# First feed-forward product of a two-layer encoder kernel: tokens stationary and 512 weight columns moving, stage borders by token tile, low weight halves in place

## The chip, the cores and the metric

The kernel runs on one core of one Trainium2 chip. The metric is the device time of one execution in microseconds (us), as the median of the runs; smaller is better. TensorE is called PE in the rows, VectorE DVE, ScalarE ACT, GpSimd POOL and SyncE SP; SPq is SP's DMA queue.

## What is computed

Two layers over 256 tokens of width 1024, in float32. Each layer is a half-weighted SwiGLU block, a mixer, and another SwiGLU block; each of the six sub-layers has an RMS norm before it, a shift and scale from a conditioning vector, and a gate on what it adds to x. Cut to what matters here:

```
def swiglu(h, w13, w2):
    a, b = jnp.split(h @ w13, 2, axis=-1)
    return (jax.nn.silu(a) * b) @ w2
...
    mod = (cond @ ada_w[layer] + ada_b[layer]).reshape(B_, N_MOD, D)
    h = modulate(rmsnorm(x, norm_g[layer, 0]), sh1, sc1)
    x = x + 0.5 * g1[:, None, :] * swiglu(h, ff_w13[layer, 0], ff_w2[layer, 0])
```

w13 is 1024 x 5632 and w2 is 2816 x 1024, each read once in each of the four feed-forward blocks. The mixer of layer 0 is two kinds of attention between an input projection (w_in) and an output projection (w_out); that of layer 1 is averaging over windows of tokens and a grouped projection (the pool stage).

## The kernel before, in words

Each engine has its own program in one fixed order, with semaphore waits written out by hand; nothing is scheduled by a compiler, so the order of the code is the order of the work. The stages are: a start (loading, the first two modulation vectors), feed-forward 0, the attention mixer, feed-forward 1, feed-forward 2, the pool stage, feed-forward 3, and the stores.

**Products in three parts.** A float32 operand is split into a high part (rounded to the PE's fast float32 form) and a low part (the rest), and a product is the sum of high x high, high x low and low x high (`three`). ACT writes the high part of a weight piece (`split_hi`, L440) and DVE the low part (`split_lo`, L694: low = raw - high). A piece is 128 x 2048 numbers, 1 MB, half of the k range for one pair of 128-column chunks; it comes by two transfers into one of 4 raw buffers, and there are 2 high and 2 low buffers. The next piece may be loaded into a raw buffer when its low part has been computed. w2 has rows of 128 x 1024 with 2 raw, 2 high and 2 low buffers (L498, L700).

**A feed-forward block** goes over 11 pairs (p = 0 to 10) of 128-column chunks. In `w13` (L1107 stands for all calls of `three`) the 128 x 128 block of weights is stationary and the 256 tokens of the transposed, normed x (`hT_hi`, `hT_lo`) move; the result u is already transposed, as w2 needs it: 48 matmuls a half, 96 a pair. ACT takes silu of the a part (L484), DVE multiplies (L708), ACT and DVE split u (L492, L714), and `w2` (L1149, L1150, L1153) multiplies with u stationary, 12 matmuls for each of two chunks Q and 24 a pair. PE's order is the first half of w13 of pair p, w2 of chunk 2p-2, the second half, w2 of chunk 2p-1.

**Beside it** run the modulation vectors of the coming stages: POOL loads rows of `ada_w` (132 transfers of 512 KB) into a ring of 4, DVE adds up (L737 for the first of 8, L740 for the others: 4 in each pair of feed-forward 0, 1 and 2, none in 3), and PE transposes the sum in every second pair (`mod_sum`, L1162), which DVE reduces (L746). A gate is spread over the tokens by PE in pair 9 (`gate_row`, L1169).

**A border between stages** (`residual`, `norm_squares`, `norm_rms`, `norm_scale`, `norm`, `norm_out`, `norm_split`): when w2 of token tile 0 (tokens 0 to 127) is done DVE multiplies by the gate and adds to x (L782, L786), ACT squares (L461; L453 for half a tile), POOL makes the reciprocal root (L358, L364), DVE scales (L795), PE transposes (L1099), ACT applies scale and shift (L472), and DVE splits into `hT_hi` and `hT_lo` (L800, L803). In PE's order the transposes of both tiles stand behind the last matmul of the stage, and the first matmul of the next stage needs both tiles of k = 0.

In the mixer PE's projection (`proj`) has 128 tokens stationary and 512 weight columns moving, 24 matmuls a piece.

## Time and profile before

| | |
|---|---|
| median of 3 runs | 1052.34 us (1050.06 to 1066.15) |
| profiled execution, span from first to last instruction | 1049.6 us |
| what lies around the span, against the median | 2.7 us |
| PE busy | 967.8 us, 92% |
| DVE busy | 737.1 us, 70% |
| ACT busy | 433.3 us, 41% |
| read from HBM | 237.54 MB, 227 GB/s over the span |

How to read it: the page does not give the profiled execution a time other than its span, so the 2.7 us are the median less that span. An engine's busy time of a matmul row includes the pipeline, so matmul rows overlap; their price is the distance between starts. The chain that ended last goes from the last instruction back to what released each step: 55% of the span stand on L1107, 21% on the three w2 lines.

### The profile page before, as it was taken

The page shows a single profiled execution, that of the slowest core. Times are in us where ns is not written, and L with a number is a line of the kernel's source. Part 1 is how long each engine was busy: PE and PEld are TensorE (multiplying, and loading weights), DVE is VectorE, ACT ScalarE, POOL GpSimd, SP SyncE. Part 2 cuts the span into 40 slices and gives each one's busy share as a digit, 9 for nine tenths or more (in the row PEclk, how much of TensorE's full clock was granted, in tenths as well). Part 3 has the DMA queues.
Part 4 walks back from the last instruction along what each step waited for, and adds up shares of the span by engine and source line. Part 5 has one row for each costly group of instructions (what it writes and reads, how often), then busy time and mean ns, then how long its engine had stood idle before and what let it go on. Part 6 is the DMA issues. An engine that isn't in the chain of part 4 may idle for free.

```text
span 1049.6 us, 15172 instructions
## 1 busy us (share of the span) xinstructions
PE 967.8 (92%) x6272; PEld 870.5 (83%) x6272; DVE 737.1 (70%) x799; ACT 433.3 (41%) x529; POOL 123.1 (12%) x182
## 2 busy tenths in 40 slices
PE   1599999998969898999999989999999879999997
PEld 1499999986757566999999979999998779999996
DVE  4888787857887636887778578978784675454543
ACT  1343434444436434443434344343443445434341
POOL 1111111002541102111110021111110010000000
PEclk9999999998989998999999989999999889999999
DMA  9989898867533015899787666989794225555621
GB/s 340 373 303 328 300 319 284 305 172 261 204 120 121 1 41 203 277 330 343 275 318 267 212 217 232 340 295 325 277 343 159 81 81 191 191 192 170 213 69 61
DMA packets 147141, 239.59 MB, mean 228 GB/s; under 512 B 16128, under 2 KB 108160, under 8 KB 146944
## 3 DMA queue, kind: packets, MB, share of 16 engines
q1 hardware_dynamic: 126480, 166.81, 47.9%
q0 software_dynamic: 19440, 71.31, 17.7%
q8 instruction: 50, 0.82, 0.3%
q10 hardware_dynamic: 1152, 0.49, 0.2%
q14 instruction: 19, 0.16, 0.0%
HBM read 237.54 MB, written 1.05 MB: 227 GB/s over the span
## 4 chain that ended last, share of the span: by engine, by line
PE 83%; DVE 10%; ACT 2%; issue 2%; POOL 1%; DMA 1%; POOLq 0%; ACTq 0%; SPq 0%; DVEq 0%
PE ps L1107 55%; PE ps L1149 7%; PE ps L1150 7%; PE ps L1153 7%; DVE x L786 1%; DVE lo L694 1%; DVE xn L782 1%; PE ps L1272 1%; PE ps L1162 1%; DVE acc L740 1%; PE ps L1169 1%; PE ps L1275 1%; DMA x<-in_x 1%; POOL rstd L364 1%; DVE xn L740 1%
## 5 line engine op out<-in xcount | busy, mean ns | idle before, releaser
L1107 PE MATMUL ps<-hT_hi,hi 128*128 128x256 f32 x1408 | 405.2, 288 | 4.4 <-DVE hT_lo L803 4.4
L1107 PE MATMUL ps<-hT_lo,hi 128*128 128x256 f32 x1408 | 401.8, 285 | 0.0
L1107 PE MATMUL ps<-hT_hi,lo 128*128 128x256 f32 x1408 | 401.5, 285 | 0.0
L694 DVE TENSOR_TENSOR lo<-raw,hi 128x2048 fp32r<-128x2048 f32 (+1 forms) x110 | 244.2, 2220 | 121.4 <-ACT hi L440 121.2
L1107 PEld LDWEIGHTS ps<-hT_hi,hi 128*128 128x128 f32 x1408 | 273.5, 194 | 9.4 <-issue 7.0
L1107 PEld LDWEIGHTS ps<-hT_lo,hi 128*128 128x128 f32 x1408 | 273.7, 194 | 3.5 <-issue 1.2
L440 ACT ACTIVATE hi<-raw 128x2048 fp32r<-128x2048 f32 (+1 forms) x106 | 200.6, 1892 | 179.5 <-PE ps L1107 162.1
L1107 PEld LDWEIGHTS ps<-hT_hi,lo 128*128 128x128 f32 x1408 | 273.5, 194 | 0.0
L1149 PE MATMUL ps<-hi,u_hi 128*128 128x512 f32 x344 | 135.3, 393 | 2.8 <-DVE u_lo L714 2.7
L1150 PE MATMUL ps<-lo,u_hi 128*128 128x512 f32 x344 | 135.1, 393 | 0.0
L347 POOL DMA_DIRECT2D ada<-in_ada_w x132 | 71.6, 543 | 438.9 <-DVE acc L740 159.8
L484 ACT ACTIVATE s_buf<-ps 128x512 f32<-128x512 f32 x44 | 26.3, 598 | 210.8 <-PE ps L1107 210.8
L700 DVE TENSOR_TENSOR lo<-raw,hi 128x1024 fp32r<-128x1024 f32 x88 | 107.3, 1219 | 8.6 <-ACT hi L498 8.6
L498 ACT ACTIVATE hi<-raw 128x1024 fp32r<-128x1024 f32 x88 | 92.4, 1050 | 39.0 <-PE ps L1153 36.5
L1153 PE MATMUL ps<-hi,u_lo 128*128 128x512 f32 x344 | 106.4, 390 | 0.0
L740 DVE SCALAR_TENSOR_TENSOR acc<-ada,cond,acc 128x1024 f32<-128x1024 f32 x73 | 93.6, 1282 | 4.5
L708 DVE TENSOR_TENSOR u_buf<-s_buf,ps 128x512 f32<-128x512 f32 x44 | 30.2, 685 | 75.8 <-ACT s_buf L484 75.8
L1149 PEld LDWEIGHTS ps<-hi,u_hi 128*128 128x128 f32 x344 | 64.9, 189 | 16.3 <-DVE u_lo L714 5.7
L1153 PEld LDWEIGHTS ps<-hi,u_lo 128*128 128x128 f32 x344 | 64.6, 188 | 14.1
L1150 PEld LDWEIGHTS ps<-lo,u_hi 128*128 128x128 f32 x344 | 64.9, 189 | 10.8
L1107 PE MATMUL ps<-hi,hT_hi 128*128 128x512 f32 (+1 forms) x144 | 58.0, 403 | 5.7 <-DVE lo L694 5.1
L492 ACT ACTIVATE u_hi<-u_buf 128x256 fp32r<-128x256 f32 x88 | 36.1, 410 | 50.0 <-DVE u_buf L708 48.5
(128 smaller groups left out, 853.0 us busy)
## 6 DMA issues: line engine op xcount, KB each, us to landing
raw<-in_ff_w SPq DMA_DIRECT2D x264, 512.0 KB, 7.0
ada<-in_ada_w POOLq DMA_DIRECT2D x132, 512.0 KB, 7.2
raw<-in_w_in SPq DMA_DIRECT2D x24, 512.0 KB, 5.1
arena<-in_ada_w SPq DMA_DIRECT2D x4, 1024.0 KB, 19.1
raw<-in_w_out SPq DMA_DIRECT2D x8, 512.0 KB, 4.3
raw<-in_ada_w SPq DMA_DIRECT2D x2, 1024.0 KB, 15.4
arena<-in_b_rpb SPq DMA_DIRECT2D x16, 128.0 KB, 4.5
x<-in_x SPq DMA_DIRECT2D x2, 512.0 KB, 7.4
```

Source lines behind the costliest of these rows:

```text
L347: pool.dma_start(ada[:, j % ADA_RING, :], ada_v[layer][:, j, v * D:(v + 1) * D]).then_inc(ada_in[j % ADA_RING], 16)
L440: nc.scalar.activation(hi, src, ACT.Copy).then_inc(hi13_done, 1)
L492: nc.scalar.activation(u_hi[:, Q % 2, :], u_buf[:, Q % 2, :], ACT.Copy).then_inc(uhi_done, 1)
L498: nc.scalar.activation(hi2[:, Q % 2, :], raw2[:, Q % 2, :], ACT.Copy).then_inc(hi2_done, 1)
L694: ins = V.tensor_tensor(lo, src, hi.bitcast(F32), ALU.subtract)
L700: V.tensor_tensor(lo2[:, Q % 2, :], raw2[:, Q % 2, :], hi2[:, Q % 2, :].bitcast(F32), ALU.subtract).then_inc(lo2_done, 1)
L708: V.tensor_tensor(u_buf[:, :, :].rearrange("p q n -> p (q n)"), s_buf[:, :, :].rearrange("p q n -> p (q n)"), ps[:, pair_bank(f, p) + 1, : ...
L740: V.scalar_tensor_tensor(dst, w, cond[:, j:j + 1], dst, ALU.mult, ALU.add).then_inc(ada_used, 1)
L1107: ins = mm(out, a, b, start=first and m == 0, stop=last and m == len(pairs) - 1, skip_group_check=shared)
L1149: mm(ps[:, 2 * t + h, :], uh, wh, start=first, stop=False)
L1150: mm(ps[:, 2 * t + h, :], uh, wl, start=False, stop=False)
L1153: ins = mm(ps[:, 2 * t + h, :], ul, wh, start=False, stop=last)
```

## The change

The code is changed in seven respects.

1. `w13` has a 128 x 128 block of normed tokens stationary and 512 weight columns moving, as two runs of 256 (the a part and the b part). A pair has 48 matmuls where it had 96. Its result has tokens on the partitions.
2. So u must be transposed before w2: `u_transpose`, four 128 x 128 PE transposes a pair, of u in float32. silu and the product work on 128 x 512 as before; the split of u now reads the transposed u from PSUM in one instruction of 128 x 512 where it had two of 128 x 256.
3. PE's order in a pair is w13 first half, transposes of u of the pair before, w13 second half, and then both chunks of w2. The modulation sums are transposed and reduced in two halves.
4. The last pair of a block and the first pair of the next are done token tile by token tile: PE does w13 and w2 of tile 0, then w13 of tile 1, the norm's transposes of tile 0, w2 of tile 1, and in the next stage w13 of tile 0 with the transposes of tile 1 in its middle. The w_out projection and the pool stage are ordered in the same way.
5. The low part of a weight is written over its raw numbers. So a raw buffer is free only when PE has used the piece, not when the low part is done.
6. The buffers saved make a ring of 4 high parts, and 4 own raw places with 3 more in the arena where the arena is free (in feed-forward 0 from piece 4 to 17, in 1, 2 and 3): the ring of 7. In the mixer and the pool stage it is a ring of 4. w2 has 4 raw places and 4 high ones.
7. DVE's order in a pair is written anew: product of the pair before, two rows of `ada_w`, a low part, a w2 low part, two rows, the low part of u, a low part, a w2 low part.

The diff, cut. Of the added functions the lines they replace stand in the kernel printed above, and are left out here.

```diff
+OWN_SLOTS, SLOTS = 4, 7
...
+ARENA_BUSY = [range(0, 4), range(18, 2 * FFN_PAIR[1]), range(76, 2 * FFN_PAIR[3])]
...
-        raw13 = sb("raw13", [P, 4, 2048])
-        raw2 = sb("raw2", [P, 2, D])
-        hi13 = sb("hi13", [P, 2, 2048], F32R)
-        lo13 = sb("lo13", [P, 2, 2048], F32R)
-        hi2 = sb("hi2", [P, 2, D], F32R)
-        lo2 = sb("lo2", [P, 2, D], F32R)
+        def sb_with_alias(name, shape, alias, alias_shape, skip=0):
+            at = (nc.sbuf_base + 31) // 32 * 32
+            return sb(name, shape), nc.alloc_sbuf_tensor_at(alias, alias_shape, F32R, offset=at + 4 * skip)
+        raw13, lo13 = sb_with_alias("raw13", [P, 4, 2048], "lo13", [P, 4, 2048])
+        raw2, lo2_all = sb_with_alias("raw2", [P, 4, D], "lo2", [P, 4, D])
+        hi13 = sb("hi13", [P, 4, 2048], F32R)
+        hi2_own = sb("hi2", [P, 2, D], F32R)
...
-                if n >= 4:
-                    sp.wait_ge(lo13_done, n - 3)
...
+                if BEFORE[n] >= 0:
+                    sp.wait_ge(unit_used, BEFORE[n] + 1)
...
-                    sp.wait_ge(lo2_done, n - 1)
...
+                if n >= 4:
+                    sp.wait_ge(w2_used, n - 3)
...
-                act.wait_ge(raw13_in[n % 4], raw13_count(n))
-                if n >= 2:
-                    act.wait_ge(unit_used, n - 1)
+                act.wait_ge(raw13_in[SLOT[n]], raw13_count(n))
+                if n >= 4:
+                    act.wait_ge(unit_used, n - 3)
...
+                nc.scalar.activation(s_buf[:, :, :], ps[:, z:z + 2, 0:256], ACT.Silu).then_inc(silu_done, 1)
...
+            def u_high(f, p):
+                act.wait_ge(uT_done, u_done_count(f, p + 1))
+                pair = PAIRS * f + p
+                if pair >= 2:
+                    act.wait_ge(w2_used, 2 * pair - 2)
+                nc.scalar.activation(u_split(pair)[0][:, :], ps[:, pair_bank(f, p), :], ACT.Copy).then_inc(uhi_done, 1)
...
+                s = SUB_OF_FFN[f] + 1
+                silu(f, LAST - 1)
+                if f < 3:
+                    split_hi(n0 + 2 * PAIRS)
+                w2_high(Q0 + NC - 3)
+                u_high(f, LAST - 1)
+                w2_high(Q0 + NC - 2)
+                silu_tile(f, 0)
+                w2_high(Q0 + NC - 1)
+                u_high_tile(f, 0)
+                if f < 3:
+                    split_hi(n0 + 2 * PAIRS + 1)
+                    norm_squares(s, 0)
+                silu_tile(f, 1)
+                if f < 3:
+                    norm_out(s, 0, 0, 4)
+                u_high_tile(f, 1)
+                if f < 3:
+                    norm_out(s, 0, 4, 8)
+                    norm_squares(s, 1, 0)
+                    norm_squares(s, 1, 1)
...
+                V.tensor_tensor(u_buf[:, :, :], s_buf[:, :, :], ps[:, z:z + 2, 256:512], ALU.mult).then_inc(u_done, 1)
...
+            def u_low(f, p):
+                dve.wait_ge(uhi_done, u_done_count(f, p + 1))
+                u_hi, u_lo = u_split(PAIRS * f + p)
+                V.tensor_tensor(u_lo[:, :], ps[:, pair_bank(f, p), :], u_hi[:, :].bitcast(F32), ALU.subtract
+                                ).then_inc(ulo_done, 1)
...
+                for p in range(LAST):
+                    g, j = FFN_MODS[min(f, 2)] + p // 2, 4 * (p % 2)
+                    sums = f < 3 and p >= 2 and p % 2 == 0
+                    if p:
+                        u_mul(f, p - 1)
+                    else:
+                        split_lo(n0 + 2)
+                    if f < 3:
                         ada_tile(g, j)
                         ada_tile(g, j + 1)
+                    split_lo(n0 + 2 * p + (2 if p else 3))
+                    if p:
+                        w2_low(Q0 + 2 * p - 1)
+                    if f < 3:
                         ada_tile(g, j + 2)
                         ada_tile(g, j + 3)
+                    if p:
+                        u_low(f, p - 1)
+                    if sums:
+                        mod_half(g - 1, 0, spare_bank(f, p) + 1)
+                    if p:
+                        split_lo(n0 + 2 * p + 3)
+                    w2_low(Q0 + 2 * p)
+                    if sums:
+                        mod_half(g - 1, 1, spare_bank(f, p) + 1)
+                    if f == 0 and p == 7:
                         mixer_setup()
+                    if (f, p + 1) in GATE_AT:
+                        k = GATE_AT[f, p + 1]
+                        diag(GATES[k], k, 1.0 if k == 4 else 0.5)
+                s, nxt, g = SUB_OF_FFN[f] + 1, n0 + 2 * PAIRS, FFN_MODS[min(f, 2)] + 4
+                u_mul(f, LAST - 1)
+                if f < 3:
+                    split_lo(nxt)
+                w2_low(Q0 + NC - 3)
+                u_low(f, LAST - 1)
+                w2_low(Q0 + NC - 2)
+                u_mul_tile(f, 0)
+                w2_low(Q0 + NC - 1)
+                u_low_tile(f, 0)
+                if f < 3:
+                    mod_half(g, 0, spare_bank(f, LAST) + 1)
+                    make_acol(s)
+                residual(s, 0, y0_done, s)
+                if f < 3:
+                    split_lo(nxt + 1)
+                    norm_scale(s, 0)
+                u_mul_tile(f, 1)
+                if f < 3:
+                    mod_half(g, 1, spare_bank(f, LAST) + 1)
+                if f < 2:
+                    norm_split(s, 0, ((0, 2), (2, 2)))
+                u_low_tile(f, 1)
+                if f < 2:
+                    norm_split(s, 0, ((4, 4),))
+                residual(s, 1, y1_half, f + 1, part=0)
+                residual(s, 1, w2_used, NC * (f + 1), part=1)
+                if f < 3:
+                    norm_scale(s, 1)
+                if f < 2:
+                    norm_split(s, 1)
...
+            def norm_transpose(s, t, first=0, last=KT):
+                pe.wait_ge(xn_done, 2 * s + t + 1)
+                for j in range(first, last):
+                    c0 = (j % 4) * P
+                    ins = nc.tensor.transpose(ps[:, norm_bank(s, t) + j // 4, c0:c0 + P], xn[:, t, j * P:(j + 1) * P],
+                                              ident[:, :])
+                    if j % 4 == 3:
+                        ins.then_inc(xT_done, 1)
...
-            def w13(f, p, half):
+            def w13(f, p, half, tiles=range(TT), between=None):
                 n = 2 * (FFN_PAIR[f] + p) + half
                 pe.wait_ge(lo13_done, n + 1)
-                for kk in range(4):
-                    k = 4 * half + kk
-                    if p == 0:
-                        pe.wait_ge(hlo_done, HLO[SUB_OF_FFN[f]] + k + 1)
-                    hh, hl = hT_hi[:, k, :], hT_lo[:, k, :]
-                    for ab in range(2):
-                        for q in range(2):
-                            c0 = (ab * 4 + kk) * 256 + q * P
-                            wh, wl = hi13[:, n % 2, c0:c0 + P], lo13[:, n % 2, c0:c0 + P]
-                            dst = ps[:, pair_bank(f, p) + ab, q * 256:q * 256 + 256]
-
-                            ins = three(dst, ((wh, hh), (wh, hl), (wl, hh)), k == 0 and q == 0, k == KT - 1, shared=True)
-                ins.then_inc(unit_used, 1)
+                wh, wl = (v.rearrange("p (m k c) -> p m k c", m=2, k=4) for v in unit_src(n)[1])
+                for t in tiles:
+                    tok = slice(t * P, (t + 1) * P)
+                    for kk in range(4):
+                        k = 4 * half + kk
+                        if p == 0:
+                            pe.wait_ge(hlo_done, HLO[SUB_OF_FFN[f]] + 8 * t + k + 1)
+                        hh, hl = hT_hi[:, k, tok], hT_lo[:, k, tok]
+                        ins = three(ps[:, pair_bank(f, p) + t, :].rearrange("p (m c) -> p m c", m=2),
+                                    ((hh, wh[:, :, kk, :]), (hh, wl[:, :, kk, :]), (hl, wh[:, :, kk, :])),
+                                    k == 0, k == KT - 1)
+                        if kk == 1 and between is not None:
+                            between()
+                    if t:
+                        ins.then_inc(unit_used, 1)
+                    elif p == LAST and half == 1:
+                        ins.then_inc(w13_t0, 1)
+            def u_transpose(f, p, tiles=range(TT)):
+                z, last = pair_bank(f, p), p == LAST
+                pe.wait_ge(u_done, u_done_count(f, p + 1 + (tiles[0] if last else 0)))
+                for t in tiles:
+                    for q in range(2):
+                        dst = ps[:, z + t, q * P:(q + 1) * P] if last else ps[:, z, q * 256 + t * P:q * 256 + t * P + P]
+                        ins = nc.tensor.transpose(dst, u_buf[:, t, q * P:(q + 1) * P], ident[:, :])
+                ins.then_inc(uT_done, 1)
...
+                Q0, s_in, s_out = NC * f, SUB_OF_FFN[f], SUB_OF_FFN[f] + 1
+                for t in range(TT):
+                    w13(f, 0, 0, [t])
+                    w13(f, 0, 1, [t], between=(lambda: norm_transpose(s_in, 1)) if f and t == 0 else None)
+                for p in range(1, LAST):
+                    g, k, spare = FFN_MODS[min(f, 2)] + p // 2 - 1, GATE_AT.get((f, p)), spare_bank(f, p) + 1
+                    sums = f < 3 and p % 2 == 0
+                    if f < 3 and p % 2 and p >= 3:
+                        pe.wait_ge(mod_red, 2 * (g + 1))
+                    if (f, p - 1) in GATE_AT:
+                        pe.wait_ge(gate_ready, 2 * GATE_AT[f, p - 1] + 2)
                     w13(f, p, 0)
+                    u_transpose(f, p - 1)
+                    if sums:
+                        mod_half(g, 0, spare)
+                    if k is not None:
+                        gate_half(k, 0, spare)
                     w13(f, p, 1)
+                    if sums:
+                        pe.wait_ge(mod_red, 2 * g + 1)
+                        mod_half(g, 1, spare)
+                    if k is not None:
+                        pe.wait_ge(gate_ready, 2 * k + 1)
+                        gate_half(k, 1, spare)
+                    w2(Q0 + 2 * p - 2)
+                    w2(Q0 + 2 * p - 1)
+                g, spare = FFN_MODS[min(f, 2)] + 4, spare_bank(f, LAST) + 1
+                w13(f, LAST, 0, [0])
+                u_transpose(f, LAST - 1)
+                w13(f, LAST, 1, [0])
                 if f < 3:
+                    mod_half(g, 0, spare)
+                w2(Q0 + NC - 4, tiles=[0], done=None)
+                u_transpose(f, LAST, [0])
+                w2(Q0 + NC - 3, tiles=[0], done=None)
+                w2(Q0 + NC - 2, tiles=[0], done=None)
+                w2(Q0 + NC - 1, tiles=[0], last=True, done=y0_done)
+                pe.wait_ge(gate_ready, 2 * GATE_AT[f, 9] + 2)
+                w13(f, LAST, 0, [1])
+                w13(f, LAST, 1, [1])
+                if f < 3:
+                    pe.wait_ge(mod_red, 2 * g + 1)
+                    mod_half(g, 1, spare)
+                    norm_transpose(s_out, 0)
+                w2(Q0 + NC - 4, tiles=[1])
+                u_transpose(f, LAST, [1])
+                w2(Q0 + NC - 3, tiles=[1])
+                if f == 2:
+                    pe.wait_ge(avg_in, 16)
+                    pe.wait_ge(mod_red, 4 * NMOD)
+                    pool_average(0, 0, 4)
+                w2(Q0 + NC - 2, tiles=[1])
+                w2_last(Q0 + NC - 1)
```

**DVE at the start of feed-forward 2.** The names are `ada` for a row of `ada_w` and `acc` for its running sum; lo, hi and raw are weight parts, u_buf is the product, u_lo the low part of u. Before, from the last split of the border on:

```order
L803 TENSOR_TENSOR hT_lo<-arena,hT_hi 128x512
L737 TENSOR_SCALAR acc<-ada,cond 128x1024
L740 SCALAR_TENSOR_TENSOR acc<-ada,cond,acc 128x1024
L694 TENSOR_TENSOR lo<-raw,hi 128x2048
L700 TENSOR_TENSOR lo<-raw,hi 128x1024
L740 SCALAR_TENSOR_TENSOR acc<-ada,cond,acc 128x1024 x2
L708 TENSOR_TENSOR u_buf<-s_buf,ps 128x512
L714 TENSOR_TENSOR u_lo<-u_buf,u_hi 128x256
```

The same place in the changed kernel (lo_49 and lo_52 are low weight parts in their raw places, lo_50 that of w2):

```order
L800 TENSOR_TENSOR lo_49<-raw,hi 128x2048
L857 TENSOR_SCALAR acc<-ada,cond 128x1024
L860 SCALAR_TENSOR_TENSOR acc<-ada,cond,acc 128x1024
L800 TENSOR_TENSOR lo_52<-arena,hi 128x2048
L860 SCALAR_TENSOR_TENSOR acc<-ada,cond,acc 128x1024 x2
L806 TENSOR_TENSOR lo_50<-raw,hi 128x1024
L814 TENSOR_TENSOR u_buf<-s_buf,ps 128x512
L860 SCALAR_TENSOR_TENSOR acc<-ada,cond,acc 128x1024 x2
L800 TENSOR_TENSOR lo_52<-arena,hi 128x2048
L806 TENSOR_TENSOR lo_50<-raw,hi 128x1024
L860 SCALAR_TENSOR_TENSOR acc<-ada,cond,acc 128x1024 x2
L819 TENSOR_TENSOR u_lo<-ps,u_hi 128x512
```

Ahead of the first product of u stand two low parts of 128 x 2048 where there was one, and ahead of the low part of u two more rows of `ada_w`, a low part and a w2 low part.

**PE at the end of feed-forward 1.** Before, the last matmuls of w2, the transposes of both tiles, and the first matmuls of feed-forward 2:

```order
L1153 MATMUL ps<-hi,u_lo 128x512 x2
L1136 MATMUL ps<-hi,u_hi 128x512
L1136 MATMUL ps<-lo,u_hi 128x512
L1136 MATMUL ps<-hi,u_lo 128x512
L1136 MATMUL ps<-hi,u_hi 128x512
L1136 MATMUL ps<-lo,u_hi 128x512
L1136 MATMUL ps<-hi,u_lo 128x512
L1099 MATMUL ps<-ident,xn 128x128 x16
L1107 MATMUL ps<-hT_hi,hi 128x256
L1107 MATMUL ps<-hT_lo,hi 128x256
```

In the changed kernel, from the last matmul of w13 for tile 1 (L1253) on: the second half of a modulation sum (L1323), the norm's transposes of tile 0 (L1245), w2 of tile 1 (L1310 to L1314) with the transposes of its u (L1286):

```order
L1253 MATMUL ps<-hi,hT_lo 128x512
L1323 MATMUL ps<-ident,acc 128x128 x4
L1245 MATMUL ps<-ident,xn 128x128 x8
L1310 MATMUL ps<-hi,u_hi 128x512
L1311 MATMUL ps<-lo_50,u_hi 128x512
L1310 MATMUL ps<-hi,u_hi 128x512
L1311 MATMUL ps<-lo_50,u_hi 128x512
L1314 MATMUL ps<-hi,u_lo 128x512 x2
L1286 MATMUL ps<-ident,u_buf 128x128 x2
L1310 MATMUL ps<-hi,u_hi 128x512
L1311 MATMUL ps<-lo_50,u_hi 128x512
```

Eight of the sixteen transposes have moved ahead of w2 of tile 1; the other eight stand in the middle of the first pair of feed-forward 2, behind 18 matmuls of its tile 0.

## Rows read from the trace of the kernel before

**Rows 1.** The page: shares of engines, then PE and its clock in 40 slices.
```profile
PE 967.8 (92%) x6272; PEld 870.5 (83%) x6272; DVE 737.1 (70%) x799; ACT 433.3 (41%) x529; POOL 123.1 (12%) x182
...
PEclk9999999998989998999999989999999889999999
```

**Rows 2.** Windows of three borders: length, busy time (count), clock, DMA share, GB/s.
```profile
230.60:247.50 16.90, 12.00 (x54) 9.06 (x53) 13.73 (x20) 8.06 (x15) 4.92 (x8) 0.83 0.68 168
603.00:619.80 16.80, 11.97 (x53) 8.99 (x52) 13.68 (x20) 7.97 (x15) 4.92 (x8) 0.82 0.38 115
809.20:851.80 42.60, 31.55 (x166) 26.91 (x164) 29.32 (x41) 20.95 (x37) 5.12 (x8) 0.85 0.16 54
```

**Rows 3.** Chain that ended last, in order of time: start, us, what.
```profile
42.81 19.45 PE ps L1107 x144
65.00 5.75 PE ps L1107 x48
73.50 5.75 PE ps L1107 x48
82.00 0.87 PE ps L1162 x8
...
247.48 11.66 PE ps L1107 x48
...
619.83 19.37 PE ps L1107 x144
641.94 5.75 PE ps L1107 x48
650.44 5.75 PE ps L1107 x48
...
1020.22 5.75 PE ps L1107 x48
```

**Rows 4.** The same chain, window 560 to 660.
```profile
587.10 5.75 PE ps L1107 x48
...
596.96 5.77 PE ps L1107 x48
```

**Rows 5.** Timeline of PE in the w_in stage, the 1st and the 25th.
```profile
252.18 0.39 PE L1107 MATMUL ps<-hi,hT_hi 128*128 128x512 f32 x1
...
257.62 0.39 PE L1107 MATMUL ps<-hi,hT_hi 128*128 128x512 f32 x1
```

**Rows 6.** Groups of instructions by form: busy us, mean ns, idle before.
```profile
L694 DVE TENSOR_TENSOR lo<-raw,hi 128x2048 fp32r<-128x2048 f32 x100 | 232.0, 2320 | 119.2 <-ACT hi L440 118.9
...
L700 DVE TENSOR_TENSOR lo<-raw,hi 128x1024 fp32r<-128x1024 f32 x88 | 107.3, 1219 | 8.6 <-ACT hi L498 8.6
...
L740 DVE SCALAR_TENSOR_TENSOR xn<-ada,cond,xn 128x1024 f32<-128x1024 f32 x42 | 53.9, 1282 | 2.5
...
L708 DVE TENSOR_TENSOR u_buf<-s_buf,ps 128x512 f32<-128x512 f32 x44 | 30.2, 685 | 75.8 <-ACT s_buf L484 75.8
...
L714 DVE TENSOR_TENSOR u_lo<-u_buf,u_hi 128x256 fp32r<-128x256 f32 x88 | 37.1, 421 | 21.3 <-ACT u_hi L492 21.3
...
L737 DVE TENSOR_SCALAR xn<-ada,cond 128x1024 f32<-128x1024 f32 x6 | 4.5, 747 | 0.0
```

**Rows 7.** Timeline of the border at 603: start, us, what.
```profile
612.61 0.68 DVE L782 TENSOR_TENSOR xn<-ps,gate 128x512 f32<-128x512 f32 x1
...
614.87 1.11 POOL L358 TENSOR_SCALAR rstd<-ss 128x1 f32<-128x1 f32 x1 [1.37 <-ACT xn L453]
...
616.66 0.75 DVE L795 TENSOR_SCALAR xn<-x,rstd 128x1024 f32<-128x1024 f32 x1 [0.84 <-POOL rstd L364]
...
617.47 1.97 PE L1099 MATMUL ps<-ident,xn 128*128 128x128 f32 x8 [0.77 <-DVE xn L795]
618.26 1.93 ACT L472 ACTIVATE arena<-ps,modc,acol 128x256 f32<-128x256 f32 x4 [3.49 <-PE ps L1099]
```

**Rows 8.** The page: transfers of the weights.
```profile
raw<-in_ff_w SPq DMA_DIRECT2D x264, 512.0 KB, 7.0
```

717 lines of the change are left out of this document (354 added, 363 removed).

## The prediction

> **What bounds the kernel now.** First the page: PE is busy 92% of the span and its clock is 9 tenths nearly everywhere, with dips [rows 1]. PE sets the time, and the dips are where it does not. Second the chain of waits in order of time: in a feed-forward block it is PE alone. A half of w13 (48 matmuls) takes 5.75 us, the next starts 8.50 us after the last began, so a pair takes 17.00 us: 11.50 for w13 and 5.50 for 24 matmuls of w2; every second pair 0.87 is added for eight 128 x 128 transposes [rows 3]. Third the windows of the borders, in which PE works only in part and at 0.82 to 0.85 of the clock [rows 2]. After the border at 603 the first 144 matmuls take 19.37 us, where 3 x 5.75 is 17.25: 2.1 us for the low clock [rows 3]. So two things can be won, PE's work in 44 pairs and the borders. DVE is second: I add up its pair below.
>
> **w13 turned round.** The 256-column matmul starts every 5.75 / 48 = 0.1198 us [rows 3]. The 512-column one with tokens stationary is in the w_in stage: 24 of them take 257.62 - 252.18 = 5.44 us, 0.2267 each [rows 5]. A pair's w13 is 48 x 0.2267 = 10.88, 0.62 less. The added transposes are four a pair at 0.87 / 8 = 0.109: 0.44 [rows 3]. Net gain 0.18, call it 0.19 with the rounding of w2; over 33 pairs away from the borders (2 to 9 of blocks 0, 1, 2; 1 to 9 of block 3) **6.3 us**. What rows do not show is the two runs of 256 that a matmul now reads. Below, nothing: it is the same count of columns. Above: each run priced as a matmul of its own, 0.2396. I take 0.2267, since count, type and stationary form are those of rows 5.
>
> The transposes also have a duration on the Trainium skill's page "TensorE: Matmul & The Clock Gate", section "Part 4: PE-mode transpose": about 275 ns each in a kernel. It speaks against this change: 176 of them would cost 48 us where I have 19, and the kernel would come out near 1066. Rows 3 show eight in 0.87 us, 109 ns from one to the next, in this kernel, in the same place between other matmuls; I follow the row, and the chances below don't use the page.
>
> **The steady pair elsewhere.** DVE's pair, by rows 6: two low parts 2 x 2.32, two of w2 2 x 1.22, four rows of ada_w 4 x 1.28, product 0.69, low part of u 128 x 512 from PSUM about 0.69 (as L708): 13.6, and about 1.6 in every second pair for the modulation sum. PE's pair is 16.8. So DVE is hidden, with 2 to 3 us to spare. ACT is busy 41% [rows 1]. The low part in place costs DVE the same read and write: zero, hidden by PE; from the other side, even 0.3 us each would stay under DVE's spare time. A raw place is freed by PE's use: with 7 places a load is issued some five pieces (40 us) ahead and lands in 7.0 us [rows 8]: zero. With 4 places in the mixer it has three pieces of 5.4 us, 16 us, for landing 7.0 and a high and a low part of at most 2.3 each: a margin of 5 at best, some 1.7 for the first piece behind the bias transfers. I take zero; at worst each of a few pieces is 2 us late.
>
> **The border at 603, step by step** (0 is the start of the last pair, 587.10 before [rows 4]). PE does tile 0 of w13 with the transposes of pair 9 by 5.9; w2 of tile 0, 24 matmuls, by 12.05; tile 1 of w13 by 17.5. Beside that DVE's residual of tile 0 (2.5), ACT's square (1.3), POOL (1.3) and scaling (0.75) end near 18.1, so PE's transposes of tile 0 run 18.2 to 19.1, warm. w2 of tile 1 ends at 24.9. By then hT of tile 0 is split, and PE goes on without a gap: the 10 us of idle and slow PE before are gone here. Tile 1 needs, from 24.9: 2.3 for the half residuals (0.68 an operation), 0.8 to square a half, 1.3 for POOL (1.1 of it can be its first operation), 0.75 to scale [rows 7]: 30.1. PE has 18 matmuls for tile 0, to 29.0, and waits 1.2; transposes to 31.1; the rest of pair 0 to 38.0.
>
> Now what is late next. DVE splits tile 1's hT until about 35.0, since ACT makes h in eight steps of about 0.35 (0.47 for twice the columns [rows 7]). Only then come, in its new order, low part 2.32, two rows 2.03, low part 2.32, two rows 2.56, w2 1.22, product 0.69: 11.1 us, to 46.1. PE wants the product for its transposes when w13's first half of pair 1 is done, at 43.4: it waits 2.8. Then transposes and second half to 52.1. DVE has rows 2.56, low 2.32, w2 1.22, rows 2.56, low part of u 0.69, 9.35 us, to 55.5: PE waits 3.5 more before w2. Behind that wait all of w2 and pair 2 are queued. Pair 1 ends at 61.1. Before, it ended at 650.44 - 587.10 = 63.3 [rows 3, 4]. **Gain 2.2**, not 8: DVE, which had its gap before, now starts each block behind. In pair 2 it has caught up.
>
> **The other places.** Start: pair 0's first matmul comes 0.4 later (42.81 before [rows 3]) since two reductions and two k blocks are waited for, tile 0's second half waits 1.0 for its low part, which now comes after norm splits, and the same DVE queue makes PE wait some 3.1 before the first w2; less 0.9 of shorter work. Pair 1 ends 76.8 against 73.5 [rows 3]; with the other rounding **loss 3.6**. Feed-forward 0 to mixer: no ada wait of that size, since only piece 24 and four rows stand ahead. The two first units of w_in end 38.3 after the last pair's start against 44.5 (247.48 + 11.66 = 259.1 [rows 3], less 214.7, which is 247.48 less the 32.7 that lie between 587.10 and 619.83 at the other border); a wait of 0.8 later eats little; the mixer behind is paced by DVE and PE in the same order, so it only shifts: **gain 6.1**. Mixer to feed-forward 1: the border is shorter by 6, then the two waits, 6.2: **0**. Pool stage: 42.6 us before [rows 2]. DVE's four differences with splits, 1.95 each, stand unchanged on the path; transposes and averages move ahead, but a low part of 2.3 now stands before the residual: tile 0 starts feed-forward 3 3 us earlier, tile 1 waits; **gain 2.5**. Feed-forward 3 has no ada rows, so no wait. End: tile 0's residual is out of the way when tile 1 is ready, 25.6 against 26.9 from 1020.22 [rows 3]: **gain 1.5**, counting its own pair.
>
> **Sum.** 6.3 - 3.6 + 6.1 + 0 + 2.2 + 2.5 + 1.5 = 15.0 us. The profiled span 1049.6 becomes 1034.6; with the 2.7 around it, as the median of before has, 1037.3.
>
> **Rivals.**
>
> *DVE is not late at the starts* (it finishes the norm earlier, or its first rows and low parts fit beside PE). Then 6.3 + 6.2 + 3.4 us of waits go: 1021.4. For it: these waits rest on hand-added times, and before, DVE waited 118.9 us in all for high parts, some of it there [rows 6]. Against: 11.1 us of DVE work stand ahead of a product that PE wants 8 us after the split.
>
> *The clock drops at the new waits.* Each of the three starts now has a gap of 2.7 and one of 3.5 us close together, and in the pool stage PE has longer ones; before, after its gap, the border's eight transposes took 1.97 us, 0.25 each [rows 7], where 0.87 is the price in a block, and the recovery cost 2.1. Four times 2.1 is 8.4: 1045.7. Against: PE is busy for 6 us between the two gaps and long before them. The skill's same page, section "HAM oscillation — how this bites in real kernels", says that work broken by repeated idle gaps starts at the half clock again after each; that would be this rival.
>
> *Slower: the two runs of 256 are paid as two matmuls.* 2112 x (0.2396 - 0.2267) = 27.2 us come on top, in every pair: 17.4 a pair in place of 17.0, and the kernel takes 1064.5, 12 more than before. It decides from 15.0 / 2112 = 7.1 ns a matmul. For it: no row has such a read. Against: the fixed part of a matmul, 0.2396 - 0.2267, looks like one of the instruction, not of the run.
>
> *Loads come late because a place is freed by use* (mixer, start): 4 to 6 pieces by 2 us, 10 us: 1047.
>
> **How the numbers follow.** Forecast 0.50, rival one 0.22, clock 0.13, slower 0.09, loads 0.06. The likeliest case's own range is 1030 to 1045. The range for 8 in 10 goes from rival one's middle to above clock and loads: 1021 to 1056. A difference of 2%, 21 us, is about what a measurement of this kernel can tell from none; the bounds are 1031.3 and 1073.4. Below 1031.3: rival one and a fifth of the forecast, 0.32. Above 1073.4: half of the slower rival, 0.05. Between: 0.63.
>
> **What would show it.** Right: w13's half at 5.44 with no gap, a pair of 16.8; four transposes in 0.44; PE's waits for the product and the low part of u once each at pair 1 of blocks 0, 1 and 2, and none in 3; a border with no PE gap over 2 us; the mixer's inner length as before. Wrong: matmul starts over 0.23 apart; PE waits for DVE in pairs 2 to 9; ACT's high part waiting for a transfer; the clock row low in pairs 0 and 1.

## The result, and the profile after

The changed kernel takes 1062.7 us (median of 20 runs, 1059.9 to 1080.7) where the kernel before takes 1052.6 beside it: a ratio of 1.0125, 95% interval 1.0102 to 1.0148. It is slower by 10 us between the medians and by 13 us by the ratio, where 15 us faster was forecast, and it lies above the range of 1021 to 1056. A ratio leaves out the executions that lie more than 1.5% above the fastest of their kernel and a median does not, so the two can differ by some us. The profiled execution has a span of 1058.6 us. These lines of its page answer to [rows 1]; the third is the DMA engines' busy share in the same 40 slices, the last the shares of the chain that ended last:

```profile
PE 960.9 (91%) x4336; PEld 774.8 (73%) x4336; DVE 736.3 (70%) x795; ACT 432.4 (41%) x555; POOL 119.2 (11%) x182
PEclk9599999999889999999999999999999989999999
DMA  9999897439743103999898539987792367656321
PE 71%; DVE 11%; DMA 5%; SPq 5%; issue 4%; ACT 3%; POOL 1%; DVEq 0%; ACTq 0%; POOLq 0%
```

PE does less work than before (960.9 us against 967.8), as the change means it to. What is new is that transfers and SyncE's queue stand on the chain, 5% each: something that PE needs now waits for a load. Where, the chain in order of time shows (start, us, what):

```profile
43.34 19.37 PE ps L1253 x72
63.15 5.49 PE ps L1253 x24
69.62 1.89 SPq L332
...
83.63 2.15 SPq L372
...
86.80 10.09 DMA raw<-in_ff_w
96.91 1.06 ACT hi L559
98.00 1.23 DVE lo L806
99.88 7.35 PE ps L1253 x24
...
118.57 5.44 PE ps L1253 x24
124.89 5.47 PE ps L1253 x24
136.29 5.44 PE ps L1253 x24
...
223.85 2.72 PE ps L1253 x12
...
249.60 1.10 SPq L393
...
265.70 11.98 DMA raw<-in_w_in
277.71 1.92 ACT hi L510
...
449.60 14.20 DMA raw<-in_ff_w
463.82 1.07 ACT hi L559
...
482.09 5.45 PE ps L1253 x24
...
604.17 2.72 PE ps L1253 x12
```

A half of w13 takes 5.44 and a pair 17.7 with a modulation sum, 136.29 - 118.57: that part is as forecast. But three times the chain runs through SP's queue into a transfer of 10 to 14 us (L332 issues a piece, L393 a part of the attention's bias). Laid beside the same points of the kernel before ([rows 3, 4] and its chain), the starts of w13 give a ledger, in us (w_out is its first 12 matmuls, 381.93 before and 394.06 after; forecast is the sum of the prediction, with the 6.3 of the pairs shared out):

| from ... to | before | after | change | forecast |
|---|---|---|---|---|
| start to pair 3 of feed-forward 0 | 91.4 | 99.9 | +8.5 | +3.4 |
| its pair 3 to its last pair | 123.4 | 124.0 | +0.6 | -1.3 |
| its last pair to w_out | 167.2 | 170.2 | +3.0 | -6.1 |
| w_out to pair 3 of feed-forward 1 | 81.8 | 88.0 | +6.2 | -0.2 |
| pair 3 to last pair, feed-forward 1 | 123.4 | 122.1 | -1.3 | -1.3 |
| last pair to pair 3 of feed-forward 2 | 81.2 | 80.6 | -0.7 | -2.4 |
| pair 3 to last pair, feed-forward 2 | 125.1 | 123.9 | -1.2 | -1.3 |
| last pair to pair 3 of feed-forward 3 | 106.1 | 102.6 | -3.5 | -2.9 |
| from there to the end | 150.1 | 147.4 | -2.7 | -2.8 |

The loss is in three places, and the waits of PE name them:

```profile
PE ps L1253 <- DVE lo L800: 11.5, 4, 8.1
...
PE ps L1310 <- DVE u_lo L819: 6.8, 2, 3.5
PE ps L1286 <- DVE u_buf L814: 4.8, 2, 2.8
...
PE ps L1253 <- DVE mraw L866: 2.9, 1, 2.9
```

Columns: us in total, times, the longest. The forecast's two waits are there (u_buf 2.8, u_lo 3.5), if not both at full length at each start. The 8.1 is new: it is the low part of piece 26, in w_in. And ScalarE's waits say what that low part (L510, a piece of w_in) and mraw (L559, the w2 rows: 9.3 us in feed-forward 0 and 13.5 in 1) had waited for:

```profile
ACT hi L559 <- DMA raw<-in_ff_w: 22.8, 2, 13.5
...
ACT hi L510 <- DMA raw<-in_w_in: 11.5, 1, 11.5
```

SyncE's own timeline shows the mechanism in feed-forward 0:

```profile
68.66 0.92 SPq L332 DMA_DIRECT2D raw<-in_ff_w  x2
69.62 13.96 SPq L332 DMA_DIRECT2D arena<-in_ff_w  x6
83.63 2.15 SPq L372 DMA_DIRECT2D arena<-in_rope_cs  x1
85.81 0.94 SPq L373 DMA_DIRECT2D arena<-in_a_lambda  x1
86.80 1.64 SPq L347 DMA_DIRECT2D raw<-in_ff_w  x1
```

When pair 1 has been used, the three arena places open at once and `load_until` issues one piece after another: five are let go by the two halves of pair 1, and the last four, eight transfers, are in the rows. Their first two need 0.92 us to issue, the next six 13.96, while the DMA engines are full (share 1.06 to 1.07, 367 to 384 GB/s from 60 to 100). The w2 rows (L347) stand behind them, and behind two small tables (L372, L373), in the one queue; they are issued at 86.8, ScalarE's high part comes at 96.9, VectorE, in its fixed order, has the modulation sum behind that row's low part, and pair 3 starts at 99.88.

### The profile page after: what moved, and what is told of

It is laid out like the page before. It is cut to its first block, busy times and chain, and to the rows that moved or that the text cites. A ratio compares the mean times of both kernels' runs of the same rounds, so it can differ in the third digit from the quotient of the medians.

```text
span 1058.6 us, 11238 instructions
## 1 busy us (share of the span) xinstructions
PE 960.9 (91%) x4336; PEld 774.8 (73%) x4336; DVE 736.3 (70%) x795; ACT 432.4 (41%) x555; POOL 119.2 (11%) x182
## 3 DMA queue, kind: packets, MB, share of 16 engines
HBM read 237.54 MB, written 1.05 MB: 225 GB/s over the span
## 4 chain that ended last, share of the span: by engine, by line
PE 71%; DVE 11%; DMA 5%; SPq 5%; issue 4%; ACT 3%; POOL 1%; DVEq 0%; ACTq 0%; POOLq 0%
PE ps L1253 41%; PE ps L1310 7%; PE ps L1311 7%; PE ps L1314 7%; SPq L332 2%; DMA raw<-in_ff_w 2%; DVE lo L800 2%; SPq L393 2%; PE ps L1286 2%; DVE acc L860 1%; PE ps L1469 1%; DMA raw<-in_w_in 1%; DVE xn L860 1%; DVE xn L901 1%; PE ps L1323 1%
## 5 line engine op out<-in xcount | busy, mean ns | idle before, releaser
L1253 PE MATMUL ps<-hi,hT_hi 128*128 128x512 f32 (+1 forms) x848 | 343.7, 405 | 19.5 <-DVE lo L800 11.5
L1253 PE MATMUL ps<-hi,hT_lo 128*128 128x512 f32 (+1 forms) x848 | 334.2, 394 | 0.0
L1253 PE MATMUL ps<-lo,hT_hi 128*128 128x512 f32 (+1 forms) x848 | 334.0, 394 | 0.0
L1253 PEld LDWEIGHTS ps<-hi,hT_hi 128*128 128x128 f32 x848 | 162.8, 192 | 59.9 <-DVE lo L800 15.5
L800 DVE TENSOR_TENSOR lo<-raw,hi 128x2048 fp32r<-128x2048 f32 (+1 forms) x76 | 174.6, 2300 | 45.0 <-ACT hi L510 45.0
L1253 PEld LDWEIGHTS ps<-hi,hT_lo 128*128 128x128 f32 x848 | 162.5, 192 | 34.5
L1253 PEld LDWEIGHTS ps<-lo,hT_hi 128*128 128x128 f32 x848 | 163.0, 192 | 33.0 <-issue 1.4
L510 ACT ACTIVATE hi<-raw 128x2048 fp32r<-128x2048 f32 (+1 forms) x76 | 143.3, 1892 | 44.5 <-DMA raw<-in_ff_w 32.9
L800 DVE TENSOR_TENSOR lo<-arena,hi 128x2048 fp32r<-128x2048 f32 x30 | 68.7, 2289 | 12.5 <-ACT hi L510 12.5
L1310 PE MATMUL ps<-hi,u_hi 128*128 128x512 f32 x172 | 70.8, 412 | 6.8 <-DVE u_lo L819 6.8
L1310 PE MATMUL ps<-arena_r 128*128 128x512 f32 x172 | 69.7, 405 | 1.4 <-DVE arena_r L819 1.4
L1311 PE MATMUL ps<-lo,arena_r 128*128 128x512 f32 x172 | 67.2, 391 | 0.0
L510 ACT ACTIVATE hi<-arena 128x2048 fp32r<-128x2048 f32 x30 | 57.3, 1911 | 0.0
L559 ACT ACTIVATE hi<-raw 128x1024 fp32r<-128x1024 f32 x44 | 46.3, 1052 | 22.8 <-DMA raw<-in_ff_w 22.8
```

The source lines that it names most:

```text
L510: nc.scalar.activation(hi, src, ACT.Copy).then_inc(hi13_done, 1)
L559: nc.scalar.activation(hi2(Q), raw2[:, Q % 4, :], ACT.Copy).then_inc(hi2_done, 1)
L800: ins = V.tensor_tensor(lo, src, hi.bitcast(F32), ALU.subtract)
L1253: ins = mm(out, a, b, start=first and m == 0, stop=last and m == len(pairs) - 1, skip_group_check=shared)
L1310: mm(ps[:, 2 * t + h, :], uh, wh, start=first, stop=False)
L1311: mm(ps[:, 2 * t + h, :], uh, wl, start=False, stop=False)
```

## The experiments

Theory L: late loads by the order of SyncE's queue. Rivals: B, the DMA engines are full whatever the order; F, places freed by use are too few; D, VectorE's order alone. Later C, the clock. Ratios are to the kernel before.

**The w2 rows ahead of the burst, and the bias ahead.**

```diff
-                    load_until(2 * (FFN_PAIR[f] + p) + 1)
+                    load_until(2 * (FFN_PAIR[f] + p) + 1, 2 * (FFN_PAIR[f] + p) + 6 if p < 2 else PIECES)
...
                         load_w2(f + 1, 1)
+                    load_until(2 * (FFN_PAIR[f] + p) + 1)
```

> The changed kernel, with only the order of SyncE's queue changed in the first two pairs of each feed-forward block: the two w2 rows are issued ahead of the burst of pieces that the freed arena places let go. Theory L (head of line: w2 rows are late because they stand behind a burst and behind waits for places in one in-order queue): in feed-forward 0 ScalarE's high part of w2 no longer waits 9 us, pair 3 starts some 6 us earlier (93 to 95 where the changed kernel has 99.9), in feed-forward 1 the wait of 13.5 us goes and pair 3 starts some 5 to 6 us earlier relative to the mixer's end, in feed-forward 2 about 1; sum 12 to 13, 1050 us. Rival B (the DMA engines are simply full there, 0.98 busy, whatever the order): another transfer is late in its place, a wait of 5 us or more for a piece or a row of ada_w appears, gain under 4, 1059 or more. Rival F (places freed by use are too few): no change, 1062.

1055.8 us, ratio 1.0064 (1.0016 to 1.0111), 6 us better than the changed kernel: half of what L gave. The high part of w2 waits 4.7 us for transfers where it was 22.8 + 2.3, pair 3 of feed-forward 0 starts at 97.7, not at 93 to 95. From w_out to pair 3 of feed-forward 1, where L gave 5 to 6 us, 87.7 are left of 88.0: with the late row gone PE waits there for VectorE instead, 3.4 and 3.0 us where it was 2.8 and 1.4. The edit hits the right thing, but something stands behind it.

The second kernel moves the 16 bias transfers from behind the block to the beginning of its last pair (`if (f, p) == (0, LAST)`).

> The changed kernel, with the 16 transfers of the attention bias issued at the beginning of the last pair of feed-forward 0 (near 216) and not after its last w2 rows (246.8 to 265). Theory L: the pieces 26 and 27 of w_in are issued when their places are free (259 and 262), not at 265, and land in 7 us or less; TensorE's wait of 8.1 us before piece 26 goes or falls under 1; the mixer behind is 8 to 9 us earlier: 1054 us. Rival F (in a ring of 4 freed by use the piece comes too late in any order): the wait stays at 6 us or more, 1060 or more. Rival B (DMA full): landing stays near 12 us, wait 4 to 6, 1058 to 1060.

1058.0 us, ratio 1.0078 (1.0023 to 1.0133). The median is what B gave, but the ten executions lie between 1050.5 and 1071.4, and the trace decides. In the trace the wait in front of piece 26 is gone altogether, as L says, and the first matmul of w_out is 7.6 us earlier. F falls for w_in: the ring of 4 is enough if its loads are issued when places open.

> Both changes of SyncE's order together. Theory L: the gains stand in different stages and add: 12 + 8.5, 1042 us, near the 1037 that was forecast with no late loads. Rival B: 1056 or more. If the two gains do not add (under 80% of their sum), something else takes the place, most likely VectorE at the start of feed-forward 1.

1053.4 us, ratio 1.0011 (0.9964 to 1.0057): 12 us back, not 20; the two gains, 6 and 5 by the ratios, add.

**The number of places.** `OWN_SLOTS, SLOTS = 4, 4`, and with it SyncE's wait for the arena ahead of the bias is left out.

> The changed kernel with 4 raw places everywhere, the three in the arena never used. Theory L: without the burst of five pieces at the first pairs the w2 rows come earlier: feed-forward 0's pair 3 starts at 93 to 96, the first pairs of feed-forward 1 lose 2 to 4 us in place of 6; steady pairs stay at 16.8; the wait before piece 26 stays near 8. Sum 6 to 10 us faster than the changed kernel, 1053 to 1057. Rival F (too few places freed by use): with 4 places it is worse in all pairs, ScalarE waits for transfers in steady pairs, and the kernel is slower than the changed one, 1065 or more. Rival B (bandwidth alone): the traffic is spread by the ring, also 1053 to 1058; told from L by the kernel with the w2 rows ahead.

1066.0 us, ratio 1.0091 (1.0048 to 1.0134), 4 us better at most. Two readings: in feed-forward 0 pair 3 starts at 94.8, 3.6 us behind the kernel before, as forecast for the start; without the burst that forecast holds. Steady pairs stay as they are, so F falls for them. What makes the time so high is something else, in the mixer; it comes below. With the loads put in order as well, four places were no better than seven:

> Four places, w2 rows and bias ahead, VectorE's order as in the changed kernel. With four_three it tells what the order is worth when loads are in time. Theory M2 (each start pays VectorE's backlog as forecast, 2.8 and 3.5 us, and on top 1.7 to 2.8 us for matmuls at the low clock behind the second wait): feed-forward 0's pair 3 starts at 94 to 95, and four_three is 6 us a start better in feed-forward 0, 1 and 2, 15 to 18 us in all; this kernel comes out at 1050 to 1052 beside 1041 to 1043. If the order is worth only the waits themselves, the difference is 16 in pieces of 5.5 a start; if under 8 in all, DMA was the limit and not VectorE.

1063.0 us, ratio 1.0102 (1.0070 to 1.0134). Pair 3 starts at 97.0, where it is 98.1 with seven places. In the profile 8.5 us of the difference to seven places stand in the mixer, whose code is the same (61.0 us from the last piece of w_in to w_out where it took 52.5): see below.

**VectorE's order at the starts.** Pairs 0 and 1 are written out: the product, the low part of u and the low parts that PE wants next, ahead of most rows.

```diff
...
+                split_lo(n0 + 2)
+                rows(0, 1)
+                w2_low(Q0)
+                u_mul(f, 0)
+                split_lo(n0 + 3)
+                rows(1, 2)
+                w2_low(Q0 + 1)
+                rows(2, 3)
+                u_low(f, 0)
+                split_lo(n0 + 4)
+                rows(3, 4)
+                split_lo(n0 + 5)
+                rows(4, 6)
+                w2_low(Q0 + 2)
+                rows(6, 8)
...
```

> The changed kernel, with VectorE's order in the first two pairs of each block rewritten: the first product and the first low part of u, and the low parts that TensorE wants next, stand ahead of most rows of ada_w (the same 8 rows are done by the end of pair 1). SyncE's order is that of the changed kernel. Theory M (the waits for u_buf and u_lo at pair 1 are VectorE's backlog, but in feed-forward 0 and 1 a second limit, the late w2 rows, lies right behind): the waits of 3.3, 2.8, 1.4, 2.0 and 3.5 us go, but pair 3 of feed-forward 0 still starts at 98 to 100 and the wait for loads grows by what was won; gain there 0 to 2, in feed-forward 2 some 6, 1055 to 1060 us. Rival D (VectorE is the only limit at the starts): all of 6 to 7 us a start comes, 1045.

1064.5 us, ratio 1.0106 (1.0052 to 1.0160): next to nothing. M expected that for feed-forward 0 and 1, where the loads are late, but 6 us in 2, and there 0.8 came (79.8 us from the last pair to pair 3, for 80.6): the waits at pair 1 are gone, and PE waits 4.6 us at pair 2 for the modulation sum.

> The w2 rows ahead, the bias transfers ahead and VectorE's new order at the starts. Theory M: with the loads in time VectorE's backlog was the only thing left at the starts; the waits of 4.7 us (feed-forward 0), 2.5 and 3.0 (1), 2.0 and 3.9 (2) go, with 1.7 to 1.9 us each of the matmuls behind them that ran at the low clock; pair 2 starts 6 us earlier in 0, 7 in 1, 7 in 2: 20 us less than with the loads alone, 1033 to 1036, faster than the kernel before by 1.5%. Rival D2 (the backlog only moves on to pair 2, to the modulation sums or the low part of its second half): under 8 us, 1045 or more.

1050.1 us, ratio 0.9968 (0.9929 to 1.0007). A miss by 15 us, of which 7 stand in the mixer again (59.6 us in the profile, 52.5 with the loads alone). In feed-forward 2 the order wins 7.2 us (81.8 to 74.6), in 0 and 1 nothing: the two waits at pair 1 are gone, but at pair 2 PE waits 2.4 us for the product and 2.6 for the sum in feed-forward 0, and 4.5 for the sum in 1.

> As the kernel with all three, but a piece is never issued more than three pairs ahead, so that the burst of feed-forward 0 is spread over its pairs. Theory L2 (what is left of late loads in feed-forward 0 is the burst itself: with 4 places its pair 3 started at 94.8, with 7 and the w2 rows ahead at 97.6 to 98.1): pair 3 starts 2 to 3 us earlier than with all three, 1031 to 1034. Rival: the places in the arena were what kept the DMA busy early, and later pairs starve: equal or slower.

1051.2 us, ratio 1.0007 (0.9976 to 1.0039). The burst is spread and nothing is won: pair 3 of feed-forward 0 starts at 100.5.

> As the kernel with all three (w2 rows ahead, bias ahead, VectorE's new order), but with 4 raw places everywhere. Theory B2 (at the starts the DMA engines are the limit: a pair needs 5 MB in 17 us, near 300 GB/s of the 380 to 390 that they reach, and filling the three extra places costs 3 MB or 8 us of them, which the rows of ada_w and the w2 rows pay): the waits for u_buf and the modulation sum at pair 2 (2.4 and 2.6 us in feed-forward 0, 4.5 in 1, 1.6 in 2) go or fall under 1; from the last pair ahead of a block to its pair 3 is 3 to 5 us shorter in 0 and 1, 1 to 2 in 2; the kernel is 7 to 10 us faster than all three, median 1041 to 1043. Rival D2 (VectorE's backlog alone makes those waits, whatever the places): they stay, within 1 us, and the time is that of all three, 1050. Rival F (four places are too few once the starts are tight): ScalarE waits for pieces, slower than all three.

1058.8 us, ratio 1.0032 (0.9995 to 1.0070). A miss: with four places the waits at pair 2 stay (4.4 us in feed-forward 1) or grow (5.9 in 2, for 1.6), so the three extra megabytes did not make them. And here F has its place after all: with VectorE's new order four places are too few. The profile is 8.7 us longer than that of all three edits with seven places, and 6.0 of them lie between the last pair and pair 3 of feed-forward 2 (80.6 for 74.6), where ScalarE waits 5.3 and 5.6 us for pieces.

> All three with 7 places, but of each row of ada_w from the third vector on only the first 512 of 1024 columns are loaded, so a pair needs 4 MB and not 5; VectorE does the same work, on numbers that are partly old. Theory B2: the waits at pair 2 for u_buf and the modulation sum go or fall under 1 in all blocks, the DMA share falls under 1 by pair 2, and the time is 7 to 10 us below all three, 1041 to 1043. Rival D2: the waits stay, 1050.

1035.7 us, ratio 0.9846 (0.9829 to 0.9864). This kernel leaves out half of each row's load, so its output is not that of the others and only its time counts. Of the 14.0 us between its profile and that of all three edits 7.7 stand in the mixer (51.9 us, where it was 59.6), and 6.3 between w_out and pair 3 of feed-forward 1 (81.0 for 87.3). There the wait for the sum shrinks from 4.5 to 0.9. In 0 the waits for product and sum are 4.8 us together where they were 5.0, and pair 3 starts no earlier (99.0, for 98.6). So the rows' traffic plays a part in 1, and in 0 it does not; VectorE's order is what is left there.

**The clock in the mixer.** These times were blurred by something that neither kernel's code explains. The 52 us from the last piece of w_in to w_out took 51.9 in the profile of before and 51.8 in that of after, but 59.6 with all three edits and 68.8 in two other kernels (the ring of 4, and only VectorE's order). The windows of 10 us (columns as in [rows 2], with PEld after PE), first of all three edits, then of the kernel with only VectorE's order:

```profile
350.00:360.00 10.00, 10.00 (x20) 4.28 (x20) 4.63 (x11) 2.16 (x9) 1.84 (x2) 0.56 0.01 2
360.00:370.00 10.00, 10.00 (x27) 5.52 (x26) 4.37 (x12) 3.72 (x11) 0.00 (x0) 0.58 0.00 0
```

```profile
353.00:363.00 10.00, 5.45 (x29) 4.09 (x27) 6.76 (x20) 5.71 (x15) 3.11 (x2) 0.79 0.01 3
363.00:373.00 10.00, 10.00 (x19) 4.50 (x18) 3.21 (x10) 1.80 (x7) 1.84 (x2) 0.50 0.00 0
373.00:383.00 10.00, 10.00 (x24) 5.29 (x23) 5.56 (x14) 2.47 (x10) 0.00 (x0) 0.50 0.00 0
383.00:393.00 10.00, 10.00 (x22) 4.87 (x21) 3.74 (x6) 4.09 (x9) 0.00 (x0) 0.50 0.00 0
```

But for the third of these windows, which holds the wait described next, PE is busy all the time at a granted clock of 0.50 to 0.58, where 0.50 is its lower level of 1.2 GHz, and does 19 to 27 matmuls in 10 us where the kernel before does 39 to 44 at 1.00. Just ahead lies a wait of 3.0 us for the softmax, in the kernel before and in all the changed ones. So 16 matmuls that nobody reads were put into that wait and the two behind it:

```diff
             qk_transpose(1, 0)
+            pe.wait_ge(win_out, 12)
+            filler(10)
             weights_transpose(3)
+            filler(3)
             values(3)
             qk_transpose(1, 1)
             pe.wait_ge(bias_done, 8)
+            filler(3)
```

> The kernel before, with 16 matmuls whose result nobody reads put into TensorE's waits in the middle of the mixer's attention (ten into the wait of 3.0 us, three and three into the next). In the profiles so far the 52 us from there to w_out took 52 in some executions, 60 or 69 in others, whose granted clock was 0.50 for 10 to 40 us behind that wait. Theory C (the clock falls because TensorE pauses there): no execution shows it, the runs lie within 3 us of each other near the lowest so far, 1047, median 1047 to 1049. Rival (the low clock comes from the chip, whatever TensorE does there): the runs spread from 1047 to 1066 as before, median 1052.

1047.4 us, from 1046.4 to 1049.2; the kernel before, run beside it, goes from 1047.1 to 1065.1 with median 1051.7. Ratio 0.9892 (0.9802 to 0.9983). C holds: filled, the pause costs nothing, and the spread is gone.

```profile
350.00:360.00 10.00, 10.00 (x37) 5.13 (x36) 7.24 (x18) 4.04 (x14) 1.84 (x2) 1.00 0.00 0
360.00:370.00 10.00, 10.00 (x46) 5.68 (x45) 7.20 (x17) 5.83 (x16) 0.00 (x0) 1.00 0.09 23
```

> The same 16 matmuls in the changed kernel. Theory C: its runs lie together near 1059, and the ratio to the kernel before with the same 16 matmuls is 1.010 to 1.013, so that the change's loss of 9 to 13 us has nothing to do with the clock in the mixer. Rival: a spread from 1058 to 1080.

1058.7 us (1055.2 to 1062.1), ratio to the kernel before as it was 1.0084 (1.0061 to 1.0107). Against the kernel before with the same matmuls it is 1058.7 / 1047.4 = 1.011: the change's loss is 11 us with the mixer's clock taken out. All further kernels have the filler.

> The changed kernel with w2 rows and bias transfers ahead and the 16 idle matmuls in the mixer, so that its low clock does not blur the comparison. Theory L: the two changes of SyncE's order are worth the 8.5 us in front of w_in's piece 26 and 2 to 3 us in front of pair 3 of feed-forward 0: 1047 to 1048, 11 less than the changed kernel with the same matmuls and level with the kernel before with them (1047.4). Rival B (DMA full, order worth little): 1052 or more.

1044.1 us, ratio 0.9898 (0.9827 to 0.9969): 14.6 us less than the changed kernel with the filler (1058.7), 3.3 less than the kernel before with it. Both of those were measured in another batch; between the profiled spans it is 11.5 and 4.3 us. So the late loads cost 11 to 15 us, L's 11 or somewhat more. That the change now wins is not clear of noise: the ratios to the kernel before are 0.9898 here and 0.9892 for the kernel before with the filler.

> The same and VectorE's new order at the starts. In the profiles, with the mixer's low clock taken out, it was worth 7.5 us, all of it in feed-forward 2 (1039.7 against 1047.3 of span). Theory M3 (the two waits at pair 1 go, but where the DMA engines are full or the modulation sum comes next, a wait at pair 2 takes their place): 1040 to 1042. Theory of the full gain, 6 a start: 1030 to 1033.

1042.7 us, ratio 0.9888 (0.9828 to 0.9948). VectorE's new order is worth 1.4 us alone: it wins 6.0 in feed-forward 2 and loses 4.4 at the start, where a wait for the modulation sum (4.1 us, and 4.6 in feed-forward 1) has come in the place of those at pair 1:

```profile
PE ps L1341 <- DVE mraw L868: 9.6, 3, 4.6
```

**Pair 2.** PE transposes the second half of a modulation sum only when VectorE has reduced the first, and that reduction stood behind four rows and the low part of u. In pair 2, where VectorE is still behind, it is moved up:

```diff
                         w2_low(Q0 + 2 * p - 1)
+                    if p == 2:
+                        if sums:
+                            mod_half(g - 1, 0, spare_bank(f, p) + 1)
+                        u_low(f, p - 1)
+                        if sums:
+                            mod_half(g - 1, 1, spare_bank(f, p) + 1)
                     if f < 3:
                         ada_tile(g, j + 2)
                         ada_tile(g, j + 3)
...
```

> The same, and two things against the waits at pair 2: VectorE reduces both halves of the modulation sum and computes the low part of u ahead of the second two rows in pair 2, and the w2 rows 2 and 3 of feed-forward 1 are loaded inside the mixer, where the DMA engines are idle. Theory M3 with its place right: the waits for mraw (2.6 us in feed-forward 0, 1.6 in 2) go with the low clock behind them, 2 to 4 us in each, and in feed-forward 1 the wait of 4.5 us shrinks by the 1 MB that is loaded earlier (2.7 us): 1032 to 1036. Rival B3 (in feed-forward 0 and 1 the rows themselves come late, the order does not matter): only feed-forward 2 gains, 1038 to 1040.

1030.4 us, ratio 0.9770 (0.9712 to 0.9829). Two edits were in it, so the order was tried without the early w2 rows, and the early rows without any of VectorE's new order:

> The fastest kernel so far (1030.4) without one of its parts: the w2 rows 2 and 3 of feed-forward 1 are again loaded at that block's start. From w_out to pair 3 of feed-forward 1 took 81.2 us with both parts and 86.4 with neither. Theory B4 (the DMA engines are the limit there, and 1 MB less at the start is worth its 2.7 us and more): 84 to 86, kernel 1033 to 1036; feed-forward 0 and 2 as in the fastest. Theory O (VectorE's order in pair 2 did it): 81 to 82, kernel 1030 to 1031.

1031.2 us, ratio 0.9722 (0.9653 to 0.9791). The ratio flatters, since the kernel before had a median of 1064.9 beside it in this batch; between the two kernels' own medians lie 0.7 us. They are level, so VectorE's order in pair 2 did it (81.6 us from w_out to pair 3, theory O), and B4 falls.

> The loads in time (w2 rows, bias) and the two w2 rows of feed-forward 1 inside the mixer, VectorE's order as in the changed kernel. Theory: the forecast's two waits, for u_buf and for the low part of u at pair 1, still stand in feed-forward 1 (2.4 and 3.0 us), since they are VectorE's; 1 MB less gives nothing there: 86 to 87 from w_out to pair 3, kernel 1043 to 1045. If the second wait is due to late rows of ada_w it shrinks by 1 us or more.

1042.1 us, ratio 0.9825 (0.9742 to 0.9908). The wait for u_buf stays at 2.6, that for the low part of u shrinks from 3.0 to 1.7. By the expectation that would be late rows, but it is not shown: in feed-forward 2, which the edit does not touch, the same wait went from 3.2 to 1.4 us.

The segments of the filled kernels, in us, between starts of w13 and w_out (the last column is the kernel without the early w2 rows):

| | before | after | loads | loads, VectorE | the same, pair 2 |
|---|---|---|---|---|---|
| start to pair 3, feed-forward 0 | 91.0 | 99.6 | 96.7 | 101.1 | 95.4 |
| last pair to w_out | 167.9 | 168.9 | 160.3 | 160.4 | 160.9 |
| w_out to pair 3, feed-forward 1 | 81.7 | 87.8 | 86.9 | 86.5 | 81.6 |
| last pair to pair 3, feed-forward 2 | 80.9 | 78.9 | 80.0 | 74.0 | 72.9 |
| last pair to pair 3, feed-forward 3 | 102.8 | 102.5 | 102.4 | 102.3 | 102.3 |

The best kernel, the change with SyncE's and VectorE's orders mended, takes 1030.4 us and is 22 us faster than the kernel before as it ran beside it, and 17 faster than that kernel with the filler, which ran in another batch.

## Why the prediction was wrong

- **w13 turned round: right.** 24 matmuls take 5.44 us (0.2267 each), two runs of 256 cost nothing, and seven pairs take 122.1 us where they took 123.4: 0.18 a pair, forecast 0.19. The rival of two runs paid as two matmuls falls.
- **Transposes: right.** The profile gives their mean as 273 ns, which is about what the Trainium skill's "TensorE: Matmul & The Clock Gate", "Part 4: PE-mode transpose", states. But that is a duration, and they overlap: four stand 0.43 apart from the transposes behind them (124.29 - 123.86 in the rows below). The price is the distance between starts.

```profile
123.86 0.60 PE L1286 MATMUL ps<-ident,u_buf 128*128 128x128 f32 x4
124.29 0.60 PE L1323 MATMUL ps<-ident,xn 128*128 128x128 f32 x4
124.65 0.48 PE L1253 MATMUL ps<-hi,hT_hi 128*128 128x512 f32 x1
```

- **"with 7 places a load is issued some five pieces (40 us) ahead and lands in 7.0 us [rows 8]: zero", and for the mixer "some 1.7 for the first piece behind the bias transfers. I take zero": this is the step that failed.** In this kernel the places were enough; the queue was not. I had priced each load by its own place, and not walked SyncE's program: a piece freed by use makes SyncE wait or burst at the moment of use, and the w2 rows and the bias stand behind. The three transfers on the chain landed in 10 to 14 us, at a DMA share of 1.05 to 1.07, where the medians of all are 5.5 and 6.1. With the filler the late loads cost 8.6 us at w_in, 2.9 at the start, 14.6 in all between medians (11.5 between the profiled spans). The rival "Loads come late" had the place and the size, 10 us, at a chance of 0.06, but as 4 to 6 pieces of 2 us each; it was one piece by 8 us and the w2 rows. The forecast's own sign of it, ACT's high part waiting for a transfer, stands in ScalarE's waits above.
- **VectorE late at the starts: the waits right, their price too small.** The waits were forecast at 2.8 and 3.5 us; with the loads in time they are 2.0 to 2.4 and 3.0 to 3.2, and in feed-forward 0 the one of 3.1 is 3.2. But they cost more than their length. Where only the order differs, feed-forward 2's start is 7.1 us shorter (80.0 to 72.9) for 5.3 us of waits, and that of 1 is 5.3 shorter (86.9 to 81.6) for 4.0 (5.4 less one of 1.4 that is left).
- **"The clock drops at the new waits": partly right.** It had a chance of 0.13 and no term. Behind the second wait of feed-forward 0 the 24 matmuls of w2 take 79.11 - 71.94 = 7.2 us, 1.7 over the 5.45 they take elsewhere, and the window of 10 us around them has 0.83. The same stands at pair 1 of feed-forward 1, where the 24 matmuls of w13 behind the wait of 2.8 us take 7.2 (447.63 to 454.79), and at its border the 24 behind the wait of 3.9 us take 6.4 (422.99 to 429.43). The Trainium skill's "TensorE: Matmul & The Clock Gate", "HAM oscillation — how this bites in real kernels", says that work broken by waits starts cold again; this trace agrees, at 1.0 to 1.7 us a time.

```profile
70.00:80.00 10.00, 8.06 (x28) 6.52 (x29) 9.03 (x8) 6.21 (x5) 2.11 (x4) 0.83 1.07 367
443.00:453.00 10.00, 7.23 (x28) 5.54 (x27) 9.79 (x8) 2.40 (x2) 2.11 (x4) 0.83 1.05 379
```

- **The borders: right into the mixer, wrong out of it, right by luck at the pool stage.** The first two units of w_in end 38.3 us after the last pair's start, as forecast (262.2 - 223.85; 262.2 is the end of the three units at 267.64 less 24 matmuls, 5.44). The pool stage's segment gives 3.5 us where 2.9 was forecast, but between the filled kernels 0.3: the kernel before took 106.1 us there in its own profile and 102.8 with the filler, which stands in another stage, at a granted clock behind the border of 0.89 and 1.00. The second step that failed is "Mixer to feed-forward 1: the border is shorter by 6, then the two waits, 6.2: 0". With the waits all but gone (one of 1.4 us is left) the segment takes 81.6 us, and 81.7 in the kernel before, so the border gave some 1.5 (an estimate from these three) and not 6. In PE's order only 18 matmuls of w_out, 4.1 us, stand between the end of tile 0's projection and its norm's transposes, and PE still waits 3.9 us for them where it waited 3.8 and 1.3 (the filled kernel before, then that with VectorE's order in pair 2):

```profile
411.30 1.40 PE L1099 MATMUL ps<-ident,xn 128*128 128x128 f32 x8 [3.79 <-DVE xn L795]
413.96 1.97 PE L1099 MATMUL ps<-ident,xn 128*128 128x128 f32 x8 [1.26 <-DVE xn L795]
```

```profile
406.31 1.97 PE L1268 MATMUL ps<-ident,xn 128*128 128x128 f32 x8 [3.94 <-DVE xn L915]
```

- **The end: right**, 1.3 us against 1.5.

With the loads in time, which the forecast took for granted, the change wins 3.3 us between medians (4.3 between spans) and not 15. The rest is in the segments of the last table: 2.3 us at the start and 1.5 at feed-forward 2, where the waits and the clock behind them cost more than forecast; 5.4 at feed-forward 1, where the waits are shorter than forecast and the border of w_out gave next to nothing; and 2.5 at the pool stage; less 1.5 that the mixer gave beyond its forecast. With VectorE's waits taken out as well it wins 17; the first rival, which left them out, had 31.

## What to carry to other kernels

When a change alters what frees a buffer, walk the queue that loads it, instruction by instruction, past every wait: a row that is small and wanted early must not stand behind a burst that is large and wanted late. Removing a wait shows the next one in the same engine's fixed order; compare stages from start to start, not waits. When a ring seems large enough, ask again after each repair: four places cost next to nothing while VectorE was late, and 9 us once it was not. A pause of 3 us in TensorE's work can cost nothing or up to 17 us behind it (51.9 to 68.8 us for the same stage), and matmuls that nobody reads are a cheap way to find out.

## What the runs showed of the hardware

- The issue of a transfer can hold up the engine that issues it while the DMA engines are full: at a share of 1.06 to 1.07 and 367 to 384 GB/s, six transfers took SyncE 13.96 us to issue, 0.51 to 3.82 each. The two just ahead took 0.92 at the same share, so the share alone does not say which issue is slow, and what holds it is not shown.
- After the wait of 3.0 us in the mixer the granted clock is 0.50 for 10 to 40 us in some profiled executions and 1.00 in others, with the same instructions of the mixer; with the wait filled it was 1.00 in each of seven, and four runs of the kernel before with the filler lay within 2.8 us where thirteen without it, beside them, spread over 18. Why PE stays so long at the lower level although it is busy is not shown. What runs there is transposes and small matmuls, and the Trainium skill says on the same page, in "Part 4: PE-mode transpose", that transposes do not count as work for the clock in the same way; no run here tests that.
